# A two-block transformer kernel: the order of loads, transposes and splits in its opening pass, with products on a zero tile added

## The reference

```
h = rmsnorm(x, norm_ffn1)            # x is 256 x 1024
x = x + 0.5 * (silu(h @ w_gate) * (h @ w_up)) @ w_down
```

## Time and profile before

| what | value |
|---|---|
| median of 3 runs | 909.7 us (909.59 to 910.04) |
| the profiled execution's own time | 910.88 us |
| its span, first to last instruction | 909.1 us |
| PE busy in the span | 885.2 us, 97% |
| mean granted clock of PE | 0.997 |
| DMA in slices of 1 us, from 3 to 23 us | 307 to 388 GB/s |

### The profile page before, as it was taken

How to read it: one execution, slowest core, us unless ns; L and a number is a source line. 1 busy time by engine, 2 the same in 40 slices (tenths; PEclk the granted TensorE clock), 3 DMA queues, 4 the chain that set the end, 5 groups by cost and what they waited for, 6 DMA issues and landing times.

```text
span 909.1 us, 14851 instructions
## 1 busy us (share of the span) xinstructions
PE 885.2 (97%) x5193; PEld 744.1 (82%) x5193; DVE 573.6 (63%) x874; ACT 479.8 (53%) x723; POOL 129.5 (14%) x111
## 2 busy tenths in 40 slices
PE   6999999999999999999999999999999999999996
PEld 5788888888677888888888878778889899999975
DVE  5655555566666556655555567889676767667665
ACT  6544444446365556544444466666646454454464
POOL 6120000010154302000000022572011000000020
PEclk9999999999999999999999999999999999999998
DMA  9796666544663325756565537452256655655511
GB/s 315 225 266 201 204 200 196 175 143 162 208 203 122 94 83 154 226 185 187 184 194 195 185 107 240 142 161 95 80 176 197 198 194 164 202 190 168 195 55 46
DMA packets 122026, 157.23 MB, mean 173 GB/s; under 512 B 10047, under 2 KB 83011, under 8 KB 121984
## 3 DMA queue, kind: packets, MB, share of 16 engines
q1 hardware_dynamic: 119648, 151.65, 52.7%
q0 software_dynamic: 1888, 4.42, 2.0%
q10 hardware_dynamic: 448, 0.59, 0.2%
HBM read 155.56 MB, written 1.07 MB: 172 GB/s over the span
## 4 chain that ended last, share of the span: by engine, by line
PE 90%; DVE 4%; ACT 3%; DMA 2%; issue 1%; SPq 0%; DVEq 0%; ACTq 0%
PE bank L504 23%; PE bank L506 23%; PE bank L505 22%; PE bank L537 4%; PE bank L536 4%; PE bank L535 4%; PE bank L618 1%; PE bank L773 1%; PE bank L959 1%; DMA w_raw<-in_w_in 1%; DMA w_raw<-in_w_ffn_up 1%; PE bank L969 1%; DVE w_lo L1866 1%; DVE w_lo L1873 1%; ACT w_hi L1317 0%
## 5 line engine op out<-in xcount | busy, mean ns | idle before, releaser
L1873 DVE TENSOR_TENSOR w_lo<-w_raw,w_hi 128x1024 fp32r<-128x1024 f32 x180 | 220.2, 1224 | 175.9 <-ACT w_hi L1326 175.9
L1326 ACT ACTIVATE w_hi<-w_raw 128x1024 fp32r<-128x1024 f32 x180 | 190.2, 1058 | 207.3 <-PE bank L506 172.4
L504 PE MATMUL bank<-w_hi,x_hi 128*128 128x512 f32 (+1 forms) x688 | 276.5, 402 | 4.6 <-DVE w_lo L1866 1.9
L506 PE MATMUL bank<-w_hi,x_lo 128*128 128x512 f32 (+1 forms) x688 | 268.1, 390 | 0.0
L505 PE MATMUL bank<-w_lo,x_hi 128*128 128x512 f32 (+1 forms) x688 | 267.6, 389 | 0.0
L504 PEld LDWEIGHTS bank<-w_hi,x_hi 128*128 128x128 f32 x688 | 129.9, 189 | 35.0 <-issue 8.6
L506 PEld LDWEIGHTS bank<-w_hi,x_lo 128*128 128x128 f32 x688 | 129.7, 189 | 27.7
L505 PEld LDWEIGHTS bank<-w_lo,x_hi 128*128 128x128 f32 x688 | 130.1, 189 | 23.8
L1866 DVE TENSOR_TENSOR w_lo<-w_raw,w_hi 128x1024 fp32r<-128x1024 f32 x84 | 105.2, 1272 | 45.0 <-ACT w_hi L1317 44.8
L1317 ACT ACTIVATE w_hi<-w_raw 128x1024 fp32r<-128x1024 f32 x100 | 103.6, 1055 | 49.9 <-PE bank L506 37.2
L504 PE MATMUL bank<-w_hi,h_hi 128*128 128x512 f32 x272 | 107.6, 396 | 1.0 <-DVE h_lo L1983 0.5
(11 more groups left out here) (310 smaller groups left out, 884.0 us busy)
## 6 DMA issues: line engine op xcount, KB each, us to landing
w_raw<-in_w_ffn_gate SPq DMA_DIRECT2D x132, 256.0 KB, 2.9
w_raw<-in_w_ffn_up SPq DMA_DIRECT2D x132, 256.0 KB, 3.1
w_raw<-in_w_ffn_down SPq DMA_DIRECT2D x132, 256.0 KB, 3.0
w_raw<-in_w_in SPq DMA_DIRECT2D x104, 256.0 KB, 3.1
w_raw<-in_w_out SPq DMA_DIRECT2D x32, 256.0 KB, 3.4
w_raw<-in_w_ple_gate SPq DMA_DIRECT2D x16, 256.0 KB, 3.4
arena<-bias_rows POOLq DMA_DIRECT2D x8, 256.0 KB, 4.6
w_raw<-in_cmp_w_k SPq DMA_DIRECT2D x8, 256.0 KB, 3.6
```

The costliest lines, as they stand in the source:

```text
L504: pe.matmul(out_, hi, wh, start=start, stop=False)
L506: return pe.matmul(out_, lo, wh, start=False, stop=stop)
L1326: act.activation(whi[:, slot * UNIT:(slot + 1) * UNIT], raw[:, slot * UNIT:(slot + 1) * UNIT], ACT.Copy).then_inc(sem("hi_done"), 1)
L1873: dve.tensor_tensor(wlo[:, s_], raw[:, s_], whi[:, s_].bitcast(F32), ALU.subtract).then_inc(sem("lo_done"), 1)
```

## The change

The loads are put in another order and on other queues; row tile 1's chunks (2 and 3) are transposed within the pass over row tile 0, after its second and fourth unit; and PE multiplies a zero tile 9 times before the first transpose and 7 times between the second chunk's transposes and the pass.

```diff
 SP
+                    if first and j >= 2:
+                        x_load(j)
...
-            for c in range(2):
-                sp.dma_start(x_chunk(c), x_rows(c)).then_inc(sem(f"x_in{c}"), 16)
-
+            sp.dma_start(rows_a[0:8, :], t["norm_ffn1"].rearrange("a (k p) -> (a k) p", p=P)
+                         ).then_inc(sem("gain0_in"), 16)
+            x_load(0)
             ffn(U_FFN1, t["w_ffn1_gate"][0], t["w_ffn1_up"][0], t["w_ffn1_down"][0], first=True)
 PE
-                tile_passes(base, (0, 1), ready=(0, 8)[f], nrm=(None, 2)[f])
+                def chunks(m, j):
+                    if m == 0 and j in (1, 3):
+                        norm_chunk(0, 2 + j // 2)
+                tile_passes(base, (0, 1), ready=(0, 8)[f], nrm=(None, 2)[f], between=None if f else chunks)
...
-                pe.wait_ge(sem("rows_in"), 16 * ROW_LOADS)
+                pe.wait_ge(sem("rows_in"), 16 * (ROW_LOADS - 4))
+                pe.wait_ge(sem("rows_act"), 16 * 4)
...
+            def warm(n):
+
+                for _ in range(n):
+                    pe.matmul(bank[0][:, :], junk[:, 0:P], junk[:, 0:512], start=True, stop=True)
+
+            pe.wait_ge(sem("warm_in"), 1)
+            warm(9)
             pe.wait_ge(sem("con_in"), 16)
             pe.wait_ge(sem("gain0_in"), 16)
             pe.transpose(bank[4][:, 0:8], rows_a[0:8, :], ident[0:8, 0:8]).then_inc(sem("gain0_full"), 1)
-            for c in range(4):
+            for c in range(2):
                 norm_chunk(0, c)
+            warm(7)
             ffn(0, U_FFN1)
 ACT
             act.dma_start(con[:, C_ID:C_ID + P], t["con"][:, C_ID:C_ID + P]).then_inc(sem("con_in"), 16)
-            act.dma_start(rows_a[0:8, :], t["norm_ffn1"].rearrange("a (k p) -> (a k) p", p=P)
-                          ).then_inc(sem("gain0_in"), 16)
-            for c in (2, 3):
-                act.dma_start(x_chunk(c), x_rows(c)).then_inc(sem(f"x_in{c}"), 16)
-            norm_hi(0, (0, 1))
+            act.dma_start(x_chunk(1), x_rows(1)).then_inc(sem("x_in1"), 16)
+            for to, r0, nr, src in row_loads[:4]:
+                act.dma_start(to[r0:r0 + nr, :], src).then_inc(sem("rows_act"), 16)
+            norm_hi(0, (0,))
             split(0)
+            norm_hi(0, (1,))
+            for v in range(1, 4):
+                split(v)
             norm_hi(0, (2,))
-            split(1)
+            for v in range(4, RING):
+                split(v)
             norm_hi(0, (3,))
-            for v in range(2, RING):
-                split(v)
             stats(0, x)
 DVE
+            dve.memset(junk[:, 0:512], 0.0).then_inc(sem("warm_in"), 1)
...
-            for c in range(3):
+            for c in range(2):
                 scaled(0, R_GAIN, c)
-            split(0)
+            for v in range(3):
+                split(v)
+            scaled(0, R_GAIN, 2)
+            for v in range(3, 5):
+                split(v)
             scaled(0, R_GAIN, 3)
-            for v in range(1, RING):
-                split(v)
+            split(5)
 POOL
-            for to, r0, nr, src in row_loads:
+            for to, r0, nr, src in row_loads[4:]:
                 pool.dma_start(to[r0:r0 + nr, :], src).then_inc(sem("rows_in"), 16)
```

More of the change, by code:

```diff
@@ L419, in load_down, with x_load @@
                                  ).then_inc(sem(f"landed{slot}"), 16)
+            def x_load(c):
+                sp.dma_start(x_chunk(c), x_rows(c)).then_inc(sem(f"x_in{c}"), 16)
             def ffn(base, wg, wu, wd, first=False, ple=None):
```

## The result

| times in us | before | changed |
|---|---|---|
| median | 910.22 us (20 runs) | 912.18 us (20 runs) |
| ratio, changed to before | | 1.0023, 95% interval 1.0017 to 1.0030 |
| profiled execution: its time, span | 910.88, 909.1 | 912.89, 911.1 |
| first real product | 11.44 | 9.69 |
| squares begin on ACT | 17.26 | 19.21 |

The change makes the kernel 2.0 us slower, 0.23% by the ratio, just beyond what I had called no change (0.2%). The opening does what the change says: PE's first real product is 1.75 us earlier and none is slow. Yet from there to unit 4 it now takes 15.8 us instead of 13.6.

A forecast was written before the change was run, and what follows sets the result against it. PE bounds the kernel before; changed, it waits for ACT's late squares, so unit 4 starts 0.8 us later. With 0.2 after it, +1.0 on the median of 909.7 gives 910.7 us, range 908.9 to 912.8.

The forecast's parts named there:

- no change: Outcome for the whole time: within 0.2% (1.8 us), between 907.9 and 911.5; chance 0.70.
- slower: Outcome for the whole time: above 911.5; chance 0.25.
- a clock that rises late: Rival: PE's clock still low in units 0 and 1, adding 2.4 us, 913.1; unit 0 alone, 911.9; chance 0.22.
- The squares' chain: From ACT's start of the squares to the end of DVE's h of row tile 0: 6.21 us, one after the other.
- PE's wait before unit 3 and before unit 4: In PE's pass: a gap released by DVE's split, then 1 us or more for DVE's h.
- PE's first product: Start of PE's pass: at 10.65, or 10.15 in the favourable case, 0.8 to 1.3 earlier.
- split 3: DVE's split within the pass: 1.21 to 2.2 us, taken as 1.45 since `x_lo` of chunk 2 overlaps part of it.
- The favourable start: Opening: transposes at the high clock, everything before ACT's first split up to 0.5 earlier; unit 4 0.5 later, not 1.0.
- the first rival: The rival of the clock rising late: low in units 0 and 1, 2.4 us added, 913.1; chance 0.22.
- The term at `bias_rows`: After unit 4, where PE reaches `bias_rows`: DVE's late columns cost 0 to 0.5 us, taken as 0.2.
- the row loads on ACT: ACT's queue in the opening: four loads, 1.7 us of issue, push the table load by about 1 us; cost nothing.
- The intended gain: PE's opening: 13 slow products made fast save 2.6 us, and the first product comes 0.8 to 1.3 earlier.

The follow-up runs named there:

- e8: The changed kernel as it is, profiled a third time in a single execution: 912.25 us.
- e12: The changed kernel as it is, timed again with a fourth profile: 912.02 us, ratio 1.0020.
- e9: The changed kernel with x chunk 0 issued ahead of the gain row: 912.08 us, ratio 1.0020.
- e5: The changed kernel with 16 zero products ahead of the pass instead of 7: 912.29 us, ratio 1.0017.
- e6: The changed kernel with the sum of squares out from behind chunk 3 and 16 zero products ahead of the pass instead of 7: 910.11 us, ratio 0.9996.
- e10: The changed kernel with early squares, 16 zero products ahead of the pass and x chunk 0 ahead of the gain row: 910.25 us, ratio 0.9999.
- e2: The changed kernel without its 16 zero products: 913.11 us, ratio 1.0026.
- e7: The changed kernel as it is, profiled once more in a single execution: 913.12 us.
- e3: The kernel before with the zero products alone added, nine before the first transpose and seven after the four chunks' transposes: 910.44 us, ratio 0.9997.
- e1: The changed kernel with the sum of squares taken out from behind chunk 3: 910.38 us, ratio 0.9994.

## Why the prediction was right, point by point

- **The range and the side.** 910.7 was forecast, in 908.9 to 912.8; 912.18 was measured. The forecast was +1.0, the measured difference is +1.96. Of the 1.48 between 910.7 and 912.18, 0.52 is the median of the kernel before (909.7 over 3 runs, 910.22 over 20) and 0.96 the change itself. My likeliest case, at 0.70, was "no change"; by my own bound of 911.5 the case that came is "slower", which had 0.25. The range held partly by luck: I had widened it upwards for a clock that rises late, and that didn't happen.
- **The mechanism holds.** The squares stand behind chunk 3, chunk 3 behind unit 3, unit 3 behind DVE. From ACT's first chunk to unit 4 I had 26.1 - 7.0 = 19.1 us. Five profiles without slow products in the pass give 25.48 - 6.47 = 19.01, e8 19.05, e12 19.01, e9 19.01, e5 19.02. With the squares early it is 17.49 in e6 and 17.51 in e10. So that place in ACT's order costs 1.5 us, and the three kernels with early squares are the three whose ratio is 1 within the interval, beside 1.0017 to 1.0026 for the changed kernel and its other variants (e2 the highest). This is shown, not only argued.
- **The seam of the pieces.** The squares' chain, 6.21 in the prediction, is 24.95 + 0.48 - 19.21 = 6.22. PE's wait before unit 3 and before unit 4 is there as forecast. From ACT's first chunk to the squares I had 19.8 - 7.0 = 12.8, and it is 12.74, but the terms between err both ways. PE's first product came 3.22 after that chunk (I had 3.65), 9.69 instead of 10.2 to 10.7. PE then waited 0.51 before unit 1, where I had 0.1. DVE's split 3 took 1.22 (I took 1.45); split 4, which I had left out of the sum, was the contended one. It ended at 18.01, and PE's transposes of chunk 3, by which my sum went, at 17.92: two paths within 0.1, so that the total is right partly by luck.
- **The favourable start failed.** I let the high clock bring ACT's first chunk forward by up to 0.5 and took 0.8 for the opening, the middle of 0.5 and 1.0. In four profiles that chunk is at 6.47, 7.14, 7.29 and 6.93, a mean of 6.96 against 7.00: no gain. In e8 the eight transposes still need 1.72 us, until 7.06; in e7 x lands at 5.64. 26.1 was nearer than 25.9 to the mean of 26.27. That mean holds one execution with five slow products, 27.33 - 7.14 = 20.19, so 1.2 us more. That is the price that I gave the first rival for one slow unit, but not its mechanism: there the clock was to be low from the start of the pass, here it had been high and fell.
- **The baseline was one execution.** I measured against 25.06. A second profile of the kernel before has 24.54, since the number of slow products isn't fixed. It is 12 in the first profile, too, and not the 13 that the prediction counts: the thirteenth, at 16.70, is followed after 0.26. The slow level cost 12 x 0.20 = 2.4 there, not 2.6. That is 0.3 of the difference in the means.
- **The term at `bias_rows`**, 0.2, is 0: unit 4 to the seam is 173.04 to 173.05 in the four profiles of the changed kernel and 173.00 and 173.02 in the two of before.
- **Loads and issues.** Unit 0 had landed by 7.01 (I had 6.95); the row loads on ACT cost nothing.
- **The intended gain.** The slow products (2.4) and a first product 1.75 earlier look like 4 us. e3 shows what the slow ones hid: with them gone PE waits for DVE's splits, and 0.3 to 0.85 is left. In the changed kernel the sum of squares takes that and more.
- **What stays open.** The opening explains 1.5 of 1.96 us. From the seam to the last scores the four profiles of the changed kernel have a mean of 124.1 and the two of before 123.5; of that 0.6, 0.4 is the one execution with the low clock near 250. The mean granted clock of every run says that the stall doesn't make the median: it is 0.996 or less in 9 of 31 runs of the changed kernel and in 10 of 79 of the kernel before, and the runs above 0.996 still have medians of 912.0 and 910.4. Whether the change makes low stretches likelier stays open, and so does where the last 0.5 us arises.

## What to carry to other kernels

When work is moved into an order by need, follow not only the operand that is wanted first but what stands last in each engine's queue: here a sum that needed only x was left behind the last chunk, and its 6.2 us chain began 1.95 us later (19.21 against 17.26). A slow stretch of the bounding engine is worth only what the engines behind it have in hand; do that sum before counting slow instructions. And one profile on either side is too few where a difference is 0.2%: the changed kernel's opening moved by 1.9 us between profiles, and a distance within the chain (first chunk to unit 4) told the kernels apart where absolute times did not.

## What the runs showed of the hardware that I had not expected

**Some operations of DVE and POOL took turns, they didn't share.** I had costed a contended split at a middling 1.45 to 1.7, as if both ran slower together. POOL and DVE of the changed kernel, in the pass and in the attention:

```profile
15.39 1.54 POOL L2778 TENSOR_TENSOR x_lo<-xg,x_hi 128x512 fp32r<-128x512 f32 x1 [4.70 <-ACT x_hi L1349]
245.42 2.39 POOL L2818 TENSOR_TENSOR w_lo<-w_raw,w_hi 128x1024 fp32r<-128x1024 f32 x1 [38.41 <-ACT w_hi L1334]
```
```profile
16.29 1.72 DVE L1884 TENSOR_TENSOR w_lo<-w_raw,w_hi 128x1024 fp32r<-128x1024 f32 x1 [0.52 <-ACT w_hi L1334]
245.93 1.92 DVE L2205 TENSOR_SCALAR arena<-arena 128x60 f32<-128x60 f32 x1 [1.01 <-ACT arena L1564]
```

DVE's split begins at 16.29, POOL's subtraction ends at 16.93, and 1.08 later, about the time of a split alone (1.22), the split is done. The operation of 60 columns at 245.93 ends at 247.85, right behind POOL's 247.81; in the kernel before the same operation took 1.22, to 246.95, behind POOL's 246.90. So each of these DVE operations got on only once POOL had finished. The Trainium skill, "SBUF — State Buffer", section "SBUF: two separate sides", says that the shared pair of ports is an exclusive lock held for a whole instruction and not a split of bandwidth. The trace agrees: 1.92 us for 60 columns that end 0.04 behind POOL. So does the mean of the squares, two columns, in e6 (DVE, then POOL): 1.25 us, ending 0.02 behind POOL, where the same operation took 0.17 in the changed kernel.

```profile
20.28 1.25 DVE L1919 TENSOR_SCALAR small<-small 128x2 f32<-128x2 f32 x1
```
```profile
19.98 1.53 POOL L2786 TENSOR_TENSOR x_lo<-xg,x_hi 128x512 fp32r<-128x512 f32 x1 [2.46 <-ACT x_hi L1351]
```

ACT's wait of 0.56 before the root in e6 comes of it, and with it most of what the early h fell short of my expectation. Not every DVE operation is held. In the kernel before, `scaled`, which reads a bank, took 0.68 in the middle of one of POOL's subtractions (2.25, until 12.42), no more than alone:

```profile
11.21 0.68 DVE L1880 TENSOR_TENSOR xg<-bank,cols_a 128x512 f32<-128x512 f32 x1
```

**The clock fell after short idle times in some executions and not in others.** In e1 and e7 PE idled for 2.1 us before unit 0, ran it fast up to its last product (0.55 and 0.54 long, in place of 0.39), waited 0.4 and then made five products at 0.43 us. So the fall came ahead of the wait of 0.4. In the changed kernel, e8, e9 and e12 the same idle time (1.93 in e8) was followed by no slow product. Where it was filled (e5, e6, e10) none was slow either, but three profiles are too few to show it as the cause. Near 250 us the level fell in the changed kernel and in e5 after waits of 1.61 and 1.25, and not in e12, e6 and e2 after 1.23, 1.28 and 1.50.

The transposes in e2 (eight in 1.97 us, then 3.2 us of idle) didn't bring the high level; 12 real products at the low one came after them. In the kernel before the last four of 16 transposes still took 1.11, against 0.66 in e3, behind zero products. The Trainium skill, "TensorE: Matmul & The Clock Gate", Part 4: PE-mode transpose, says that transposes don't count as busy time of PE in the same way. The trace agrees with it as far as these rows go, and with nine zero products ahead the level was high by 5.9 in the changed kernel.
